# Two output-projection jobs moved into the sample attention's block of a streaming encoder layer

## What is computed

```python
z  = u @ w_in + b_in       # -> q, k, v of two attentions, gate_a, gate_b
oa = differential_attention(...)   # 1024 wide
ob = chunk_band_attention(...)     # 512 wide
m  = sigmoid(gate_a) * (oa @ p_a) + sigmoid(gate_b) * (ob @ p_b)
x  = LN1(alpha * x + gate1 * (m @ w_out))
u2 = LN(x) * (1 + scale2) + shift2
x  = LN2(alpha * x + gate2 * (shared(u2) + routed_experts(u2)))
```

## Time and profile before

| what | value |
|---|---|
| median of 3 runs | 1316.66 us (1316.28 to 1318.08) |
| the profiled execution, its own time | 1306.64 us |
| its span, first to last instruction | 1304.9 us |
| mean granted TensorE clock | 0.927 of full |
| PE busy | 1023.1 us (78%) |
| DVE, ACT, POOL busy | 428.7, 239.5, 217.9 us |
| DMA moved | 347.50 MB, mean 266 GB/s |

### The profile page before, as it was taken

How to read it: one execution, slowest core, us unless ns; L and a number is a source line. 1 busy time by engine, 2 the same in 40 slices (tenths; PEclk the granted TensorE clock), 3 DMA queues, 4 the chain that set the end, 5 groups by cost and what they waited for, 6 DMA issues and landing times.

```text
span 1304.9 us, 23540 instructions
## 1 busy us (share of the span) xinstructions
PE 1023.1 (78%) x8385; PEld 652.9 (50%) x8386; DVE 428.7 (33%) x815; ACT 239.5 (18%) x478; POOL 217.9 (17%) x361
## 2 busy tenths in 40 slices
PE   4899999966785799983787778787877887756865
PEld 3898878855664344532344444344433444433432
DVE  4533343448643113783411111111121112101118
ACT  3322223325454000120011111110100111100110
POOL 0011000002200000101222222222232232212211
PEclk9899999979898899996789899989898999988988
DMA  9575545456272991185679699987999988899955
GB/s 349 171 255 184 186 131 183 169 187 221 75 268 68 327 277 65 45 362 155 234 269 385 251 398 394 364 293 300 406 374 388 335 305 303 327 397 402 404 211 233
DMA packets 97815, 347.50 MB, mean 266 GB/s; under 512 B 14961, under 2 KB 20129, under 8 KB 73050
## 3 DMA queue, kind: packets, MB, share of 16 engines
q1 hardware_dynamic: 81162, 311.56, 64.4%
q0 software_dynamic: 13856, 30.13, 6.9%
q10 hardware_dynamic: 2736, 4.98, 1.1%
HBM read 329.15 MB, written 29.52 MB: 275 GB/s over the span
## 4 chain that ended last, share of the span: by engine, by line
PE 27%; DMA 16%; issue 6%; DVE 2%; SPq 1%; ACT 0%; POOL 0%; POOLq 0%; DVEq 0%; ACTq 0%
PE PS L1826 8%; DMA hT<-h_rows,ixo 7%; DMA W<-w 7%; PE PS L1841 6%; PE PS L1857 4%; PE PS L1882 4%; PE PS L1896 2%; PE PS L1832 1%; DMA vec<-ln_b 1%; PE PS L1814 1%; PE PS L1872 1%; DVE hido L1948 0%; PE PS L1849 0%; DVE hid L1943 0%; DMA W<-expert_rows 0%
## 5 line engine op out<-in xcount | busy, mean ns | idle before, releaser
L1826 PE MATMUL PS<-W,XT 128*32 128x256 f32 x2048 | 128.4, 406 | 51.0 <-DMA W<-w 27.9
L1841 PE MATMUL PS<-W,XTo 128*64 128x256 f32 x1216 | 140.7, 384 | 0.0
L1826 PEld LDWEIGHTS PS<-W,XT 128*32 128x32 f32 x2048 | 79.5, 117 | 115.1 <-issue 90.2
L1841 PEld LDWEIGHTS PS<-W,XTo 128*64 128x64 f32 x1216 | 94.0, 138 | 44.9 <-issue 11.7
L1857 PE MATMUL PS<-W,hidTo 128*64 128x512 f32 x304 | 88.5, 707 | 16.3 <-DVE hidTo L1951 10.7
L306 PE MATMUL PS<-w_hi,u_hi 128*128 128x512 f32 x240 | 94.1, 392 | 1.2 <-DVE w_lo L432 0.7
L306 PE MATMUL PS<-w_hi,u_lo 128*128 128x512 f32 x240 | 93.5, 389 | 0.0
L306 PE MATMUL PS<-w_lo,u_hi 128*128 128x512 f32 x240 | 93.4, 389 | 0.0
L1882 PE MATMUL PS<-W,hidT 128*32 128x512 f32 x512 | 69.3, 654 | 26.8 <-issue 24.9
L432 DVE TENSOR_TENSOR w_lo<-raw,w_hi 128x2048 fp32r<-128x2048 f32 x26 | 59.5, 2289 | 91.9 <-ACT w_hi L372 91.9
L1911 ACT ACTIVATE sg<-PS 64x256 f32<-64x256 f32 x32 | 12.1, 378 | 343.4 <-PE PS L1826 343.4
(11 more groups left out here) (342 smaller groups left out, 1488.6 us busy)
## 6 DMA issues: line engine op xcount, KB each, us to landing
W<-w SPq DMA_DIRECT2D x192, 1024.0 KB, 13.1
raw<-w_in SPq DMA_DIRECT2D x26, 1024.0 KB, 5.3
wada<-w_ada SPq DMA_DIRECT2D x6, 2048.0 KB, 7.6
W<-expert_rows SPq DMA_DIRECT2D x24, 512.0 KB, 12.6
kc<-cache_k_diff SPq DMA_DIRECT2D x8, 512.0 KB, 5.1
vc<-cache_v_diff SPq DMA_DIRECT2D x8, 512.0 KB, 3.6
Wa<-p_a SPq DMA_DIRECT2D x4, 1024.0 KB, 7.4
Wa<-w_out SPq DMA_DIRECT2D x4, 1024.0 KB, 10.0
```

The lines of the kernel that those rows point to most:

```text
L1826: mm = pe.matmul(PS[64 * h + 32 * c:64 * h + 32 * c + 32, UP_B + i, 0:F], XT[:, i, k, 32 * c:32 * c + 32], t.W13[:, 2 * i + c, h, k], star ...
L1841: mm = pe.matmul(PS[64 * h:64 * h + 64, XH_B, 0:F], XTo[:, k], t.W13[:, slot, h, k], start=k == 0, stop=k == KD - 1)
```

## The change

- The waits for the first block's DRAM writes (modulation, keys, values, gates) go from the end of the first block to the end of POOL's list in `attention_prompt`.
- One tile `middle` holds the two bias tiles, `V`, later the experts' `W2`, and, laid over the biases and over the first tiles of `V`, p_a's left half (`wa0`) and p_b's left half (`wb0`), `gated` behind them, and a small tile of the shared expert.
- In `attention_sample`, SP issues `wa0` (two DMAs of 1 MB) behind the values of stream 2 and `wb0` (1 MB) behind those of stream 3. PE does job 0 between the joining matmuls and the transposes of the norm's result, and job 1 after these, as its last work in the block.
- In `projection_out`, SP begins with the gates of jobs 0, 1, 2; the 3 MB of left halves are gone. PE begins with job 2. Jobs 0 and 1 are in banks 4 to 7, the others in banks 0 to 3. The order of all else stands.

```diff
 # condition_and_project
+        t.written = [(mod_out[i], 64 * (MOD_Z // 2)) for i in range(2)] + [(k_out[0], 96), (k_out[1], 48), (v_out, 16 * NT * len(VC))]
+        t.written += [(g_out[i], 16 * NT * len(GC) // 2) for i in range(2)]
...
-            for i in range(2):
-                act.wait_ge(g_out[i], 16 * NT * len(GC) // 2)
 # attention_prompt, end of POOL's list
+            for signal, count in t.written:
+                pool.wait_ge(signal, count)
 # attention_sample, SP, end of the loop's body
+                if b == 2:
+                    for h in range(2):
+                        sp.dma_start(t.wa0[:, 4 * h:4 * h + 4], half_of(t.p_a, h)).then_inc(t.wa0_in[h], 16)
+                if b == 3:
+                    sp.dma_start(t.wb0, t.p_b[0].rearrange("(k p) n -> p k n", p=P)[:, :, 0:CW]).then_inc(t.wb0_in, 16)
 # attention_sample, PE, behind the joining matmuls
+            for h in range(2):
+                pe.wait_ge(t.wa0_in[h], 16)
+            pe.wait_ge(t.wb0_in, 16)
+            project_first(pe, t, 0)
             pe.wait_ge(on_done, 1)
             pe.wait_ge(sot_ev, 2)
             for n in range(2):
                 for i in range(4):
                     mm = pe.transpose(PS[:, n, P * i:P * i + P], On[:, 4 * n + i], t.ident[:, :])
                 mm.then_inc(sot_mm, 1)
+            project_first(pe, t, 1)
...
+def project_first(pe, t, n):
+    q, bank = slice(P * n, P * n + P), 4 + 2 * n
+    for k in range(KD):
+        pe.matmul(t.PS[:, bank], t.oaT[:, k, q], t.wa0[:, k], start=k == 0, stop=k == KD - 1)
+    for k in range(DB // P):
+        pe.matmul(t.PS[:, bank + 1], t.obT[:, k, q], t.wb0[:, k], start=k == 0, stop=k == DB // P - 1)
 # projection_out, SP
-            for c in range(2):
-                cols = slice(CW * c, CW * c + CW)
-                sp.dma_start(Wa[:, c, 0:4], half_of(t.p_a, 2 * c)).then_inc(wa_in[c], 16)
-                sp.dma_start(Wa[:, c, 4:8], half_of(t.p_a, 2 * c + 1)).then_inc(wa2_in[c], 16)
-                sp.dma_start(Wb[:, c], t.p_b[0].rearrange("(k p) n -> p k n", p=P)[:, :, cols]).then_inc(wb_in[c], 16)
-                if c == 0:
-                    for m in range(NT):
-                        load_gates(m)
+            for m in range(NT):
+                load_gates(m)
+            sp.dma_start(Wa[1][:, 0:4], half_of(t.p_a, 2)).then_inc(wa_in[1], 16)
+            sp.dma_start(Wa[1][:, 4:8], half_of(t.p_a, 3)).then_inc(wa2_in[1], 16)
+            sp.dma_start(Wb[1], t.p_b[0].rearrange("(k p) n -> p k n", p=P)[:, :, CW:2 * CW]).then_inc(wb_in[1], 16)
...
-                sp.wait_ge(p_mm, NT * (c + 1))
+                sp.wait_ge(p_mm, NT * (c + 1) - FIRST)
 # projection_out, PE and DVE (FIRST is 2)
-                if m >= 2:
+                if m >= FIRST + 2:
                     pe.wait_ge(m_ev, m - 1)
...
-            for m in range(2 * NT):
+            for m in range(FIRST, 2 * NT):
                 project(m)
                 if m > NT:
                     turn(m - NT - 1)
...
-                dve.wait_ge(p_mm, m + 1)
+                if m >= FIRST:
+                    dve.wait_ge(p_mm, m - FIRST + 1)
                 dve.wait_ge(gt_in[m % NT], 32 * (m // NT + 1))
```

More of the change, by code:

```diff
@@ L1150, in projection_out @@
         U2 = sb("U2", [P, NT, D])
-        Wa = sb("Wa", [P, 2, KD, CW])
-        Wb = sb("Wb", [P, 2, DB // P, CW])
+        Wa = [t.wa0, sb("Wa1", [P, KD, CW])[:, :, :]]
+        Wb = [t.wb0, sb("Wb1", [P, DB // P, CW])[:, :, :]]
         G = sb("gates_sb", [P, NT, 2, CW])
-        gated = sb("gated", [P, 2, CW])
+        gated = t.gated
         gate1, shift2, scale2 = sb("gate1", [P, 2, D]), sb("shift2", [P, 2, D]), sb("scale2", [P, 2, D])
@@ L1169, in projection_out @@
         block = ctx.enter_context(nc.Block())
-        jobs = [(c, n) for c in range(2) for n in range(NT)]
+        jobs, FIRST = [(c, n) for c in range(2) for n in range(NT)], 2
+        bank_of = lambda m: 4 + 2 * m if m < FIRST else 2 * (m % 2)
         @block.sync
@@ L1202, in _ @@
             for c in range(2):
-                sp.wait_ge(p_mm, NT * (c + 1))
-                sp.dma_start(Wa[:, c, 0:4], half_of(t.w_out, 2 * c)).then_inc(wa_in[c], 16)
-                sp.dma_start(Wa[:, c, 4:8], half_of(t.w_out, 2 * c + 1)).then_inc(wa2_in[c], 16)
+                sp.wait_ge(p_mm, NT * (c + 1) - FIRST)
+                sp.dma_start(Wa[c][:, 0:4], half_of(t.w_out, 2 * c)).then_inc(wa_in[c], 16)
+                sp.dma_start(Wa[c][:, 4:8], half_of(t.w_out, 2 * c + 1)).then_inc(wa2_in[c], 16)
             for n in range(NT):
@@ L1214, in project @@
                 c, n = jobs[m]
-                if m >= 2:
+                if m >= FIRST + 2:
                     pe.wait_ge(m_ev, m - 1)
                 q = slice(P * n, P * n + P)
-                pe.wait_ge(wa_in[c], 16)
+                if c:
+                    pe.wait_ge(wa_in[c], 16)
                 for k in range(KD):
-                    if k == 4:
+                    if c and k == 4:
                         pe.wait_ge(wa2_in[c], 16)
-                    pe.matmul(PS[:, 2 * (m % 2)], t.oaT[:, k, q], Wa[:, c, k], start=k == 0, stop=k == KD - 1)
-                pe.wait_ge(wb_in[c], 16)
+                    pe.matmul(PS[:, bank_of(m)], t.oaT[:, k, q], Wa[c][:, k], start=k == 0, stop=k == KD - 1)
+                if c:
+                    pe.wait_ge(wb_in[c], 16)
                 for k in range(DB // P):
-                    mm = pe.matmul(PS[:, 2 * (m % 2) + 1], t.obT[:, k, q], Wb[:, c, k], start=k == 0, stop=k == DB // P - 1)
+                    mm = pe.matmul(PS[:, bank_of(m) + 1], t.obT[:, k, q], Wb[c][:, k], start=k == 0, stop=k == DB // P - 1)
                 mm.then_inc(p_mm, 1)
@@ L1245, in out @@
                 for c in range(2):
-                    pe.wait_ge(wa_in[c], 32)
-                    pe.wait_ge(wa2_in[c], 32)
+                    pe.wait_ge(wa_in[c], 16 + 16 * c)
+                    pe.wait_ge(wa2_in[c], 16 + 16 * c)
                     for k in range(KD):
-                        mm = pe.matmul(PS[:, 2 * (n % 2) + c], MT[:, k, P * n:P * n + P], Wa[:, c, k], start=k == 0, stop=k == KD - 1)
+                        mm = pe.matmul(PS[:, 2 * (n % 2) + c], MT[:, k, P * n:P * n + P], Wa[c][:, k], start=k == 0, stop=k == KD - 1)
                 mm.then_inc(y_mm, 1)
@@ L1445, in routing @@
         none, place, dest = sb("none", [P, NBLK]), sb("place", [P, NBLK]), sb("dest_r", [P, NBLK], I32)
-        sh_g, sh_h, sh_T = sb("sh_g", [P, 2, F]), sb("sh_h", [P, NT, F]), sb("sh_T", [P, 2, 2, P])
+        sh_g, sh_h, sh_T = sb("sh_g", [P, 2, F]), sb("sh_h", [P, NT, F]), t.turned_shared
         mask_done, rank_mm, cnt_mm, code_done, list_mm = (sem(x) for x in
@@ L2114, in streaming_layer @@
         t.load_mod = load_mod
+        biases = 2 * HA * 256
+        middle = scoped(ctx, "middle", [P, biases + NT * (DA + DB)])
+        t.alibi_p = middle[:, 0:HA * 256].rearrange("p (h x) -> p h x", h=HA)
+        t.band_p = middle[:, HA * 256:biases].rearrange("p (h x) -> p h x", h=HB)
+        t.V = middle[:, biases:].rearrange("p (n d) -> p n d", n=NT)
+        t.wa0 = middle[:, 0:KD * CW].rearrange("p (k n) -> p k n", k=KD)
+        t.wb0 = middle[:, biases:biases + DB // P * CW].rearrange("p (k n) -> p k n", n=CW)
+        t.gated = middle[:, biases + DB // P * CW:biases + DB // P * CW + 2 * CW].rearrange("p (i n) -> p i n", i=2)
+        t.W2 = middle[:, 0:WB * 2 * D].rearrange("p (e j d) -> p e j d", e=WB, j=2)
+        t.turned_shared = middle[:, WB * 2 * D:WB * 2 * D + 4 * P].rearrange("p (i j q) -> p i j q", i=2, j=2)
+        t.wa0_in = [ctx.enter_context(nc.semaphore(f"wa0_in{i}")) for i in range(2)]
+        t.wb0_in = ctx.enter_context(nc.semaphore("wb0_in"))
         t.oaT = scoped(ctx, "oaT", [P, HA, TOK])
@@ L2162, in streaming_layer @@
             t.W13 = scoped(scope, "W13", [P, WB, 2, KD, F])
-            t.W2 = scoped(scope, "W2", [P, WB, 2, D])
             routing(nc, t)
```

9 lines of the change are left out of this document (1 added, 8 removed).

## The result

The kernel is slower. Median 1323.53 us of 10 runs (1313.33 to 1337.04), against 1312.02 us for the kernel before in 10 runs (1309.60 to 1319.15); the ratio is 1.0066, 95% interval 1.0035 to 1.0097, or +8.7 us (4.6 to 12.7). The ratio is of means, without two of the ten runs (1333.17 and 1337.04 us), which the chip ran in a slower state, so it is smaller than that of the medians. The forecast was +5.8 us, 1.0044 as a ratio. Single runs of one kernel scatter by 10 us and more, so most of what follows is read from the traces, stage by stage.

What follows compares the result with a forecast made beforehand. The projection's first stretch was taken as bound by PE and, with half a microsecond to spare, by the DMA queue. -1.9 + 4.0 + 9.6 - 8.1 + 2.2 = +5.8 us: 1312.4 profiled, 1322.5 median; range about -1.9 to +13.7.

Steps and rivals of the forecast that it cites:

- Write waits moved: First block's end: ACT's wait for its last gate write goes, and the whole rest moves earlier; -1.9 us.
- Loads in the loop: Sample loop: three added 1 MB loads ahead of the next keys stall PE; +4.0 us (0 to 8.4).
- Jobs 0 and 1 in the tail: Sample loop's tail: job 0 hidden under the norm, job 1 hidden by nothing; +9.6 us.
- 3 MB less in the queue: Projection: job 3's gates come earlier only by the queue time of the removed loads, PE waits some 19 us; -8.1 us.
- Restart: Projection: after idling 19 us PE restarts at the lower clock, covered by nothing; +2.2 us (0 to 4.4).
- gates in time: Rival: gates land before PE ends job 4, so PE alone bounds the projection; 1300.6 us; chance 0.18, wholly or in part.
- Wash: Rival: the sample loop's loads cause no stall and the projection's restart loses no clock; -0.4 us, 1316.3; chance 0.13.
- Lower clock: Rival: the clock falls before jobs 0 and 1 run in the tail, each taking 20.6 us; 1343.1 us; chance 0.03.

Runs made afterwards that it cites:

- e3: The changed kernel with only the one tile and the moved write waits, all six jobs and loads back in the projection; ratio 1.0002 to the kernel before.
- e1: The changed kernel with the gates of jobs 3 to 5 issued ahead of x and the vectors; 1319.22 us, ratio 1.0049 to the kernel before.
- e2: As e1, plus w_out's left half right behind those gates and its right half ahead of the router's weights; 1307.75 us, ratio 0.9972.
- e5: The changed kernel with the three loads in the sample loop moved from streams 2 and 3 to streams 6 and 7; 1318.08 us, ratio 1.0055.
- e4: The changed kernel with job 1 back in the projection's block, only job 0 kept in the sample block; 1314.56 us, ratio 1.0017.
- e6: Control: the kernel before the change, with e2's order of SP's queue; 1317.36 us, ratio 1.0052 to the kernel before.
- e8: As e7, with the right halves of p_a and p_b issued ahead of the first gates; 1309.89 us, ratio 0.9986 to the kernel before.
- e9: As e7, with w_out's right half issued ahead of shift2 and scale2; 1301.45 us, ratio 0.9925 to the kernel before.
- e7: The changed kernel with the edits of e2 and e5 together; 1302.78 us, ratio 0.9935 to the kernel before.
- e10: As e7, but only job 0 in the sample block and job 1 back in the projection; 1299.89 us, ratio 0.9889.

## Why the prediction was right, and where its sizes were off

The direction and the places held, and so did the mechanisms but for one stall in the loop; the time lies in the range. Term by term, with the measured value behind the forecast one:

- *Write waits moved:* -1.9, measured -1.75. As said; e3 shows it alone.
- *Loads in the loop:* +4.0, measured +4.87. The first stall was forecast at 3.6 and is 3.87 (3.45 in e1, 5.01 in e2). The second (0.9, p_b ahead of the keys of stream 5) didn't come. In its place the clock fell at the first, which the prediction held only as an upper end of the restart: 0.93 of the remaining 1.00 us are the transposes at 1.97 instead of 1.04. That the sum of the term came out near is partly luck. e5 shows that the cost is the loads' place.
- *Jobs 0 and 1 in the tail:* +9.56, measured +9.75; job 0 hidden and at full clock (e4: 0.12), job 1 by nothing. The joining matmuls end at 410.52 + 1.94 = 412.46, not at about 412.1 as the prediction reads; that alone is more than the 0.2 by which the term is off.
- *3 MB less in the queue:* -8.07, measured -7.23: job 3's gates were there 489.71 - 440.26 = 49.45 us behind the block's first DMA, forecast 48.6. SP was held 12.01 instead of 11.39 us by the shared weights; the other 0.2 us I don't place, and with the same loads ahead of them the gates came 49.98 us behind it in e5 and 51.73 in e4, so this miss is within the scatter. PE's wait: 19 forecast, 20.07 measured.
- *Restart:* +2.2, measured +2.33 (from the transposes behind job 4 to the first w_out matmul 506.39 - 491.77 = 14.62, before 496.84 - 484.55 = 12.29). The restart that priced it had not followed the 9.34 us of idleness, as the prediction says, but the 7.11 us wait for p_a behind it.

PE's first matmuls with w_out before, from which the restart is reckoned:

```profile
496.84 7.03 PE L1249 MATMUL PS<-Wa,MT 128*128 128x512 f32 x16
```

The terms make +7.97, 2.2 more than forecast, of which the loop has 0.9, the queue 0.8, the tail 0.2, the write waits and the restart 0.3. With the measured terms the change's share agrees with the runs' +8.7 (4.6 to 12.7). That the median, 1323.53, lies within about 1 us of the forecast 1322.5 is luck: the forecast was added to the median of three runs of before, 1316.66, and that of ten is 1312.02. The pair of profiles differs by 15.4 in span: another 1.17 before the change's first effect, 0.41 in the prompt attention, 0.7 in the rest up to the experts and 5.1 in the experts' stage. There PE's busy time and clock are the same in both (519 us, 0.91), and that stage varies by up to 11.2 us from profile to profile. The two kernels without the arena are among the three shortest there (701.6, and 703.3 in e6), e3 has 704.4; I take most of the 5.1 for scatter, and what causes it stays open.

The rivals: *gates in time* did not come by itself, but e2 made it come: it gave 15.0 of the 21.9 us that lie between that rival and the forecast; its two short waits for weights, with the slow matmuls behind them, cost some 8 us, which covers the rest. *Wash* failed on both its conditions (3.87 us of stall, a restart at 0.50). *Lower clock* failed: job 0 began 1.87 us after the joining matmuls started, at full clock.

On keeping PE busy: the tail rose from 30% to 94% busy and the kernel became slower. The Trainium skill (Perfetto Trace Analysis, Optimizing DMA Performance, Optimization Strategies) gives as the general goal to use the matmul engine as highly as possible, and where it idles for others, to work on those that block it. Read of the tail, its first half says that the change should have paid, and the trace disagrees (over the whole execution PE's busy time hardly moved: 1023.1 of 1304.9 us before, 1024.7 of 1320.3 after); its second half is what e2 did (-15.0 us in the projection), and there the trace agrees.

## What to carry to other kernels

Work moved into a gap is worth what the wait behind its old place gives up, not its own duration: before moving it, follow the first wait behind that place to its queue, and move that queue's order in the same change. In an in-order queue, price each insertion by the slack of the next load behind it (here 1.8 us of slack against 5.4 us of transfer), and put it behind the last tight load. When a wait is removed, look for the next thing in the same queue before counting the gain: three of these ten runs (e1, e8, e9) only moved a wait.

## What the runs showed of the hardware that was not expected

Some short waits cost twice. Behind waits of 0.77 to 1.09 us for p_a (e9, e5, e7) job 3's matmuls with p_a ran at full clock (7.13 us in e5 and e7); behind 2.19 us in e2 they took 8.83, and the granted clock there:

```profile
449.00:453.00 4.00, 1.80 (x5) 0.59 (x4) 1.92 (x2) 0.00 (x0) 0.00 (x0) 0.98 1.01 377
453.00:457.00 4.00, 4.00 (x7) 1.63 (x6) 0.00 (x0) 0.00 (x0) 0.00 (x0) 0.59 1.05 387
457.00:461.00 4.00, 4.00 (x10) 1.71 (x9) 0.00 (x0) 0.00 (x0) 0.00 (x0) 1.00 1.05 388
```

The loss of 1.8 us is nearly as long as the wait. In e2 the granted clock is 1.00 through the whole wait (450.20 to 452.30) and up to 452.80, and 0.50 from 453.30 to 456.00: it fell when PE was at work again. Losses of 1.8 to 3.0 us came behind 2.43, 2.92, 4.72 and 5.90 us of waiting for w_out (8.80, 8.80, 10.07, 9.19 us instead of 7.03).

The broadcast rows are slow by themselves. In before and after the shared expert's weights are issued close behind them, within the slow stretch (188 and 181 GB/s), so either could be the cause. In e7 these are issued only at 482.44, and the 10.0 MB ahead of the rows (gates, right halves, w_out's left half, x), at 390 GB/s from about 437, are through near 462. From there:

```profile
457.00:461.00 4.00, 4.00 (x10) 1.71 (x9) 1.92 (x2) 0.00 (x0) 0.00 (x0) 1.00 1.06 401
461.00:465.00 4.00, 4.00 (x11) 1.76 (x10) 0.00 (x0) 0.00 (x0) 0.00 (x0) 1.00 1.04 364
465.00:469.00 4.00, 4.00 (x17) 2.28 (x16) 1.24 (x2) 0.84 (x2) 0.00 (x0) 1.00 1.04 213
469.00:473.00 4.00, 4.00 (x10) 1.73 (x10) 0.68 (x1) 0.24 (x1) 0.00 (x0) 1.00 1.03 235
473.00:477.00 4.00, 4.00 (x11) 1.72 (x10) 0.00 (x0) 0.00 (x0) 0.00 (x0) 1.00 0.58 205
477.00:481.00 4.00, 4.00 (x17) 2.28 (x16) 1.92 (x2) 1.07 (x2) 0.00 (x0) 1.00 0.63 190
```

At a share of 1.04 they move 213 to 235 GB/s, then 205 and 190 at a share near 0.6, so the later rows leave a part of the DMA engines idle; why, no run shows. An estimate from these windows: 4 MB of rows cost the time of 7 to 8 MB of weights at 390 GB/s. That is why what stands close behind them in the queue was late in e2, e6, e7 and e10.

Ahead of them the stream ran at 401 GB/s. The Trainium skill (DMA: Bandwidth & Descriptors, Specifications) gives about 358 GB/s as a core's limit from HBM; here, with one core at work, the windows lie above it, as they did before.
